# Compressed keys and values: high and low parts of a token block in one stationary operand of 120 columns

## What is computed

```python
n_cmp = (T - CMP_BLOCK) // CMP_STRIDE + 1            # 15 blocks of 32 tokens, one every 16 tokens
tok = jnp.arange(n_cmp)[:, None] * CMP_STRIDE + jnp.arange(CMP_BLOCK)[None, :]

def compress(raw, j):                                # j = 0: keys, j = 1: values
    blk = raw[:, tok] + cmp_pos[j][None, None, :, None, :]
    blk = blk.transpose(0, 1, 3, 2, 4).reshape(B, n_cmp, N_KV_HEADS, CMP_BLOCK * HEAD_DIM)
    hid = jax.nn.gelu(blk @ cmp_w1[j] + cmp_b1[j])   # 60 rows x 2048 times 2048 x 256
    return hid @ cmp_w2[j] + cmp_b2[j]
```

## Time and profile before

| | |
|---|---|
| median of 3 runs | 1018.43 us (1018.09 to 1018.6) |
| span of the profiled execution | 1018.0 us |
| PE busy | 994.2 us, 98% of the span |
| DVE busy | 802.1 us, 79% |
| ACT busy | 539.3 us, 53% |
| chain that ended last, by engine | PE 85%, DVE 6%, DMA 3%, ACT 2%, issue 2%, SP's queue 2% |
| PE's three product lines L1970 to L1972 | 1096 products each, 312.1, 310.1 and 310.1 us |
| the compression's lines L2266, L2267, L2268 | 32 products each, 9.1, 8.9 and 9.0 us |

### The profile page before, as it was taken

One profiled execution on the slowest core, in us unless ns is written; L12 is line 12 of the kernel. 1 busy time (PEld: TensorE's weight loads), 2 busy tenths in 40 slices (PEclk: granted clock), 3 DMA queues, 4 the chain that ended last, 5 costly groups with the idle time before them and its releaser, 6 DMA issues.

```text
span 1018.0 us, 16927 instructions
## 1 busy us (share of the span) xinstructions
PE 994.2 (98%) x6901; PEld 877.0 (86%) x6901; DVE 802.1 (79%) x1208; ACT 539.3 (53%) x706; POOL 76.1 (7%) x80
## 2 busy tenths in 40 slices
PE   6999999999999999999999999999999999999997
PEld 3687799989987999887889999988999789999996
DVE  2459799868988987867978878872789799878796
ACT  4354644345446557766545454465764765454544
POOL 0000000000000000000630000000790000000000
PEclk9999999999999999999999999999999999999999
DMA  9999699969997998002999777725434286555511
GB/s 340 386 386 366 227 336 397 334 235 364 328 343 261 281 375 319 2 2 85 393 348 310 269 279 284 250 80 165 126 125 151 99 288 209 195 177 194 179 42 42
DMA packets 130333, 243.60 MB, mean 239 GB/s; under 512 B 6587, under 2 KB 95312, under 8 KB 124112
## 3 DMA queue, kind: packets, MB, share of 16 engines
q1 hardware_dynamic: 125616, 238.77, 66.6%
q10 hardware_dynamic: 4639, 3.76, 1.3%
HBM read 239.37 MB, written 1.05 MB: 236 GB/s over the span
## 4 chain that ended last, share of the span: by engine, by line
PE 85%; DVE 6%; DMA 3%; ACT 2%; issue 2%; SPq 2%; DVEq 0%; ACTq 0%
PE bank L2038 26%; PE bank L1970 13%; PE bank L1971 13%; PE bank L1972 13%; PE bank L2050 3%; DMA raw<-in_a_w_in_dram 1%; SPq L653 1%; DVE wlo L1198 1%; PE bank L2323 1%; DMA raw<-in_b_w_in_dram 1%; PE bank L2349 1%; PE bank L1864 1%; PE bank L2519 1%; DVE hcat L1338 1%; PE bank L2361 1%
## 5 line engine op out<-in xcount | busy, mean ns | idle before, releaser
L1198 DVE TENSOR_TENSOR wlo<-raw,whi 128x2048 fp32r<-128x2048 f32 x143 | 328.6, 2304 | 49.9 <-ACT whi L723 48.1
L723 ACT ACTIVATE whi<-raw 128x2048 fp32r<-128x2048 f32 x144 | 274.1, 1904 | 146.0 <-PE bank L2038 76.1
L1970 PE MATMUL bank<-hcat,whi 128*128 128x256 f32 x1096 | 312.1, 285 | 1.0 <-DVE wlo L1198 0.9
L1971 PE MATMUL bank<-hcat,whi 128*128 128x256 f32 x1096 | 310.1, 283 | 0.0
L1972 PE MATMUL bank<-hcat,wlo 128*128 128x256 f32 x1096 | 310.1, 283 | 0.0
L1970 PEld LDWEIGHTS bank<-hcat,whi 128*128 128x128 f32 x1096 | 210.1, 192 | 7.6 <-issue 3.0
L1971 PEld LDWEIGHTS bank<-hcat,whi 128*128 128x128 f32 x1096 | 210.2, 192 | 1.4
L1972 PEld LDWEIGHTS bank<-hcat,wlo 128*128 128x128 f32 x1096 | 210.1, 192 | 0.0
L1817 DVE SCALAR_TENSOR_TENSOR cvt<-ut,vec,cvt 128x189 f32<-128x189 f32 (+2 forms) x176 | 68.2, 429 | 20.9 <-ACT cvt L1161 18.4
L2038 PE MATMUL bank<-whi,fhi 128*128 128x512 f32 x240 | 75.0, 394 | 0.0
L2038 PE MATMUL bank<-wlo,fhi 128*128 128x512 f32 x240 | 74.1, 390 | 0.0
(11 more groups left out here) (432 smaller groups left out, 1631.1 us busy)
## 6 DMA issues: line engine op xcount, KB each, us to landing
raw<-in_ada_w_dram SPq DMA_DIRECT2D x40, 1024.0 KB, 8.6
raw<-in_ff_w_in_dram SPq DMA_DIRECT2D x32, 1024.0 KB, 7.4
raw<-in_ff_w_out_dram SPq DMA_DIRECT2D x32, 1024.0 KB, 7.1
raw<-in_w_ada_dram SPq DMA_DIRECT2D x24, 1024.0 KB, 6.4
raw<-in_w_up_dram SPq DMA_DIRECT2D x22, 1024.0 KB, 5.1
raw<-in_w_in_dram SPq DMA_DIRECT2D x12, 1024.0 KB, 5.4
raw<-in_w_down_dram SPq DMA_DIRECT2D x11, 1024.0 KB, 4.8
raw<-in_ada_w_dram SPq DMA_DIRECT2D x16, 512.0 KB, 12.1
```

Of the source, the lines that this page charges most:

```text
L723: act.activation(whi[:, m % SPL, 0:w], raw[:, pl.nm[m] % RAW, 0:w], ACT.Copy).then_inc(s_hi, 1)
L1198: dve.tensor_tensor(wlo[:, m % SPL, 0:w], raw[:, pl.nm[m] % RAW, 0:w], whi[:, m % SPL, 0:w], ALU.subtract).then_inc(s_lo, 1)
L1970: pe.matmul(dst, wh[:, kt, n], ah[:, kt, :], start=kt == 0, stop=False)
L1971: pe.matmul(dst, wh[:, kt, n], al[:, kt, :], start=False, stop=False)
```

## The change

For each piece, the 60 high and the 60 low columns now lie side by side in `bw[j]`, and PE takes all 120 as one stationary operand. One product with `whi` gives in one bank the rows high by `whi` (0 to 59) and low by `whi` (60 to 119); a second product with `wlo` adds high by `wlo` and low by `wlo`. The two halves of the rows are added when they are turned: ACT copies 120 rows to `ht`, and in place of the transpose stands a product with `fold`, two 60x60 identities one above the other. DVE makes `fold` once, from two slices of `ident`. The copy of the 68 ones is gone. The numbers of lines shift by one to three.

```diff
-    ht = r("ht", [NG * NC, 2, T])
+    WIN = NG * NC
+    ht = r("ht", [2 * WIN, 2, T])
+    fold = r("fold", [2 * WIN, WIN])
...
-    WIN = NG * NC
-    bw = [sb(f"bw{j}", [P, 2 * 16 * WIN + P - WIN], F32R, (oS, oK + 8192)[j]) for j in range(2)]
+    bw = [sb(f"bw{j}", [P, 16, 2, WIN], F32R, (oS, oK + 8192)[j]) for j in range(2)]
...
-                    act.activation(ht[:, j, :], ps[j][0:WIN, 0:T], ACT.Copy).then_inc(s_ht, 1)
+                    act.activation(ht[:, j, :], ps[j][0:2 * WIN, 0:T], ACT.Copy).then_inc(s_ht, 1)
...
-                    high, low = (bw[j][:, 16 * WIN * i:16 * WIN * i + 16 * WIN].rearrange("p (i w) -> p i w", w=WIN) for i in range(2))
+                    high, low = bw[j][:, :, 0, :], bw[j][:, :, 1, :]
+                    if j == 0:
+                        dve.tensor_tensor(fold[:, :], ident[0:2 * WIN, 0:WIN], ident[0:2 * WIN, WIN:2 * WIN], ALU.add)
...
-                    dve.tensor_copy(bw[j][:, 32 * WIN:32 * WIN + P - WIN], one1[:, 0:P - WIN])
...
-                            k = (8 * c + i) * WIN
-                            ah, al = bw[j][:, k:k + P], bw[j][:, 16 * WIN + k:16 * WIN + k + P]
-                            pe.matmul(ps[j][:, 0:T], ah, wh[:, i, :], start=c == 0 and i == 0, stop=False)
-                            pe.matmul(ps[j][:, 0:T], ah, wl[:, i, :], start=False, stop=False)
-                            mm = pe.matmul(ps[j][:, 0:T], al, wh[:, i, :], start=False, stop=c == 1 and i == 7)
+                            both = bw[j][:, 8 * c + i, :, :].rearrange("p a w -> p (a w)")
+                            pe.matmul(ps[j][0:2 * WIN, 0:T], both, wh[:, i, :], start=c == 0 and i == 0, stop=False)
+                            mm = pe.matmul(ps[j][0:2 * WIN, 0:T], both, wl[:, i, :], start=False, stop=c == 1 and i == 7)
...
-                        mm = pe.transpose(ps[2 + j][:, WIN * nt:WIN * nt + WIN], ht[:, j, P * nt:P * nt + P], ident[0:WIN, 0:WIN])
+                        mm = pe.matmul(ps[2 + j][:, WIN * nt:WIN * nt + WIN], ht[:, j, P * nt:P * nt + P], fold[:, :], start=True, stop=True)
```

## The result

The changed kernel takes 1021.13 us (median of 8 runs, 1019.91 to 1023.01), the kernel before beside it 1018.53 us (8 runs, 1018.09 to 1020.23). The ratio is 1.0021, with a 95% interval of 1.0012 to 1.0030; it is taken over the runs, and is not the quotient of the two medians (1.0026). The forecast was 1018.5 us with a range up to 1020.2: the median lies 0.9 us above the range. Two more comparisons on other chips, of 11 runs each, gave 1.0017 [1.0008, 1.0026] and 1.0019 [1.0010, 1.0027], a third 1.0009 [1.0000, 1.0019]. The change costs 1 to 2 us.

What follows compares the result with a forecast made beforehand. PE was busy 98% of the span, but around the compression the second query tile's load bounded it. Minus 3.8 us of products, plus 3.8 of waits, plus 0.03 of fold kept the span at 1018.0: forecast 1018.5 us, range 1017.3 to 1020.2.

Steps and rivals of the forecast that it cites:

- Products: Compression on PE: 96 products become 64, still 0.118 us apart with 120 columns, 3.8 us less work on PE.
- Where the 3.8 us go: Four compression tiles on PE: removed time becomes waits, 0.70 growing to 3.7 us ahead of the second query tile; gain 0.
- DVE: Copies, cast, subtraction and sum into `fold`: between 0.2 us shorter and 0.8 us longer, covered by waits.
- The fold: Four transposes become full products before the gates: 0.21 us more on PE, 0.18 covered by ACT's Gelu, 0.03 left.
- The clock: Rival at the new 3.7 us wait: PE's clock falls, query tile starts at half rate; 1.6 or 3.2 us more.
- The sum, zero: Whole span: minus 3.8 us of products, plus 3.8 of waits, plus 0.03 of fold; stays at 1018.0 us.
- the rival with a chance of 0.19 in all: Clock falling in the wait ahead of the query tile: one low stretch 1020.1 us (0.13), two 1021.7 us (0.06).
- the new wait is shorter, which speaks for a clock that holds: Clock argument: the new 3.7 us wait is under the 5.2 us that the full clock outlasted after the last product.
- The starting point: Forecast base: the profiled execution's 1018.0 us span, with the median of the runs shown taken as 0.4 us above it.
- The other rivals: Load earlier, 1017.4 us (0.05); attention's low stretch gone, 1016.8 (0.04); both, 1015.8 (0.03); products further apart, 1021.3 (0.02).
- That the attention's stretch might go with the change: Rival in the attention: its low clock stretch disappears, minus 1.6 us, 1016.8 us; chance 0.04 alone, 0.03 with the earlier load.

Runs made afterwards that it cites:

- after_last: The changed kernel with no edit, timed and profiled again: 1021.16 us, ratio 1.0019 [1.0010, 1.0027] against the kernel before.
- after_look2: The changed kernel with no edit, the second of two single profiled executions: 1020.26 us, beside 1018.37 us of the kernel before.
- after_again: The changed kernel with no edit, timed in five rounds and profiled again: 1020.62 us, ratio 1.0009 [1.0000, 1.0019] against the kernel before.
- after_look1: The changed kernel with no edit, the first of two single profiled executions: 1020.87 us, beside 1018.37 us of the kernel before.
- after_more: The changed kernel with no edit, timed and profiled again: 1021.35 us, ratio 1.0017 [1.0008, 1.0026] against the kernel before.
- after_swap1: The changed kernel with only the `ada` load ahead of the second query tile issued behind it: 1020.16 us, ratio 1.0012 [1.0003, 1.0021].

## Why the prediction was wrong, step by step

*Products, right.* 64 products remain, 0.12 us apart (360.86 to 360.98). The load of a 120-column operand takes 181 ns at the median, as the line through 48 and 128 columns gave. There was no fast load to lose. On the rule of the Trainium skill ("TensorE: Matmul & The Clock Gate", on weight-path perf modes) trace and page agree: the page excludes FP32, and the trace lists these operands as f32. So the page did not speak against the change, as the prediction had it.

*Where the 3.8 us go, right.* The fourth tile's rounding starts at 363.10 (said: 363.0), DVE's multiply-add at 367.27 (367.3), the fourth tile on PE at 367.40 (367.4), its last product at 369.28 (an end of 369.3 was said), the query tile at 372.94 (373.0). The gain of 0 on the path came true to 0.06 us. One of these numbers is partly luck. The prediction let ACT's rounding of the fourth tile wait for PE's last product of the first tile; that product starts at 362.54, and what ended the wait now was the tile's own load:

```profile
363.10 1.92 ACT L724 ACTIVATE whi<-raw 128x2048 fp32r<-128x2048 f32 x1 [0.76 <-DMA raw<-in_cmp_w_dram]
```

*DVE, right.* The cast takes 662 ns and the subtraction 1160 ns on the new layout, against 660 and 1153; the sum into `fold` takes 213 ns.

*The fold, too small, without effect.* The four products come as eight records: from the first to the gate product behind them it is 0.81 us (378.80 to 379.61), where the transposes took 0.38 (378.95 to 379.33). That is 0.43 us more, against 0.21 as the upper bound. ACT's Gelu covered 0.18 of it, as was said, and another 0.15 did not show because the fold began that much sooner than the transposes had (378.80 against 378.95), which nobody had counted on: L2290 starts at 382.38 in place of 382.30, 0.08 us later in place of 0.03.

*The clock, where it failed.* The sum, zero, held; the rival with a chance of 0.19 in all was what happened. The step that failed is the sentence "the new wait is shorter, which speaks for a clock that holds". It took the end of the program, where the clock outlasted 5.2 us without a product, as a bound for a wait in the middle. Four of six profiled executions fell at a wait of 3.3 to 3.4 us. One execution that holds is no bound: the first profile of the changed kernel held too. Even at the end of the program the 5.2 us were one case among others. In the first execution of the changed kernel the last product there ends at 1011.17, and the clock falls 2.0 us later:

```profile
1010.78 0.39 PE L2052 MATMUL bank<-whi,clo 128*128 128x512 f32 x1
```

```profile
1012.00:1013.00 1.00, 0.00 (x0) 0.00 (x0) 0.97 (x3) 0.29 (x1) 0.00 (x0) 1.00 0.48 178
1013.00:1014.00 1.00, 0.00 (x0) 0.00 (x0) 0.96 (x4) 0.00 (x0) 0.00 (x0) 0.57 0.93 346
```

Over all 14 profiled executions of this record, the one of before among them, this time lies between 2.0 us (this one) and 5.4 us (after_last). A wait of 3.4 us lies inside that spread, which fits a clock that holds in some executions and falls in others. The Trainium skill ("TensorE: Matmul & The Clock Gate", "Why this matters for your kernels") warns against long idle gaps between bursts of products; four of the six executions bear it out and two don't, and the one row that the prediction set against it was too little.

*The sizes of that rival, about right.* One stretch was put at 1.6 us and 1020.1 us in all, two at 1021.7 us. At the query tile a stretch cost 1.5 us (after_look2) and a long one 2.7 us (after_again); the runs at 0.996 to 0.997 (single stretches, short or long) have a median of 1020.62 us, those at 0.995 and less one of 1021.70 us. The chances were far off: the forecast, a time without such a fall, had 0.67, and 1 of 41 runs came without a low stretch.

*The starting point, wrong by the way.* The profiled execution of before already had a low stretch in its attention (span 1018.0 us, clock 0.997), and I set it equal to a median of 1018.43 us. In all 13 profiled executions that show both, the time is 1.8 to 2.0 us above the span, so that this execution took an estimated 1019.9 us, like the 37 runs of the middle column and not like the 50 of the first. "One stretch more" should have been counted from a usual run without any. It changes no step, but it hid that the kernel before is mostly at full clock and has that to lose.

*The other rivals.* In the six executions of the changed kernel the load landed between 368.35 and 369.63, at best 0.35 us sooner than before, and the products kept their distance. That the attention's stretch might go with the change: runs without any low stretch have become rarer, not more frequent; three of the six profiled executions did have none in the attention, but those had fallen at the wait.

## What to carry to other kernels

Ahead of a wait for a transfer, removed products are worth nothing by themselves, and less than nothing if the idle time grows long enough for the clock to fall behind it: first pull the transfer forward, and all that the same engines have queued behind the next transfer, then remove the products. Before calling a change neutral, look at the granted clock of many runs, since one profile can show the clock held where most executions lose it. Where a wait can't be ended, products of zeros in it can keep the clock: here seven, in the first half of it, were enough.

## What the runs showed of the hardware that I had not expected

The same kernel with the same wait of 3.3 to 3.4 us kept the clock in two executions and lost it in four, at different points: 1.0 us ahead of the tile's first product in after_look1, 1.5 us after it in after_look2. It then stayed low for 3.4 us (after_more, after_look2) or 6.8 us (after_again, after_look1). With 1.6 us of idle time in place of 3.4, and with 2.35 us in after_swap1, the profiles show one execution each, the first held and the second fallen (1.0 us after PE was back at work); 7 of the 11 timed runs with 1.6 us had no low stretch. In both executions in which the clock held at the wait it fell in the attention, with PE shown busy all the time (3.00 of 3.00 us from 439 to 442); what brings on that fall stays open. The kernel before has it too: 37 of its 87 runs show a single low stretch by their clock, and in its one profile it lies in the attention.
